# Four places where one stage of a transformer kernel hands over to the next: order of matmuls, norm steps and operand splits changed

## The reference

```
def _layer(x, g_pre, g_post, w_in, ..., w_out, row, col):
    h = _rms_norm(x, g_pre)
    proj = jnp.einsum('bsd,de->bse', h, w_in)
    ...                                        # attention heads o_a, o_b, o_c
    y = jnp.einsum('bse,ed->bsd', jnp.concatenate([o_a, o_b, o_c], axis=-1), w_out)
    return x + _rms_norm(y, g_post)
```

## Time and profile before

| | |
|---|---|
| runs | 2911.41, 2913.14, 2915.44 us; median 2913.14 us |
| profiled execution | 2914.45 us, its span 2912.8 us |
| PE | busy 2877.8 us, 99% of the span |
| PEld / DVE / ACT / POOL | 2472.4 / 2123.5 / 1316.2 / 399.9 us |
| chain that ended last | PE 85%, DVE 5%, DMA 5%, ACT 2% |
| DMA | 620.59 MB, mean 213 GB/s |

### The profile page before, as it was taken

The page is one execution under the profiler, slowest core; times in us unless marked ns, Lnnn a source line. Parts: engine busy times, 40 slices in busy tenths (PEclk is TensorE's granted clock), DMA queues, the critical chain, the costliest instruction groups (busy, mean ns, idle before and its releaser), DMA issues.

```text
span 2912.8 us, 42860 instructions
## 1 busy us (share of the span) xinstructions
PE 2877.8 (99%) x15946; PEld 2472.4 (85%) x15946; DVE 2123.5 (73%) x2854; ACT 1316.2 (45%) x1677; POOL 399.9 (14%) x390
## 2 busy tenths in 40 slices
PE   9999999999999999999999999999999999999998
PEld 7888788888888888988888888888888888887886
DVE  6697776687776857877588787448874488888745
ACT  5443544443543334755355444444444444444433
POOL 1134010133021101020088200000000000000001
PEclk9999999999999999999999999999999999999999
DMA  9867477866568867266455444555445454445543
GB/s 344 306 214 274 177 255 276 303 228 248 194 224 287 302 251 257 80 245 224 168 188 188 187 182 178 189 197 185 179 175 200 187 188 178 174 181 180 193 190 144
DMA packets 100413, 620.59 MB, mean 213 GB/s; under 512 B 11088, under 2 KB 11216, under 8 KB 38096
## 3 DMA queue, kind: packets, MB, share of 16 engines
q1 hardware_dynamic: 71360, 509.88, 47.0%
q0 software_dynamic: 28944, 109.26, 10.6%
HBM read 616.99 MB, written 2.10 MB: 213 GB/s over the span
## 4 chain that ended last, share of the span: by engine, by line
PE 85%; DVE 5%; DMA 5%; ACT 2%; issue 1%; POOL 1%; SPq 0%; POOLq 0%; DVEq 0%; ACTq 0%
PE ps L586 27%; PE ps L1057 17%; PE ps L596 14%; PE ps L540 14%; PE ps L1133 6%; DMA aring<-in_ada 5%; DVE wl L2001 2%; PE ps L1015 1%; DVE aring L2017 1%; ACT BIG L1223 1%; ACT wh L1223 1%; PE ps L778 1%; PE ps L818 0%; PE ps L894 0%; PE ps L698 0%
## 5 line engine op out<-in xcount | busy, mean ns | idle before, releaser
L1223 ACT ACTIVATE wh<-ring 128x2048 fp32r<-128x2048 f32 (+2 forms) x499 | 895.0, 1800 | 1272.7 <-PE ps L596 645.9
L2001 DVE TENSOR_TENSOR wl<-ring,wh 128x2048 fp32r<-128x2048 f32 (+1 forms) x433 | 990.0, 2287 | 482.4 <-ACT stage_h L1223 249.7
L586 PE MATMUL ps<-hhl,wh 128*128 128x512 f32 x3680 | 884.6, 392 | 0.2 <-ACT wh L1223 0.2
L586 PEld LDWEIGHTS ps<-hhl,wh 128*128 128x128 f32 x3680 | 677.1, 189 | 132.5 <-issue 0.9
L596 PEld LDWEIGHTS ps<-hhl,wl 128*128 128x128 f32 x3680 | 471.6, 191 | 19.6 <-DVE wl L2001 1.9
L596 PE MATMUL ps<-hhl,wl 128*128 128x256 f32 x3680 | 477.5, 283 | 0.7 <-DVE wl L2001 0.6
L540 PE MATMUL ps<-wh,hhl 128*128 128x512 f32 (+1 forms) x1728 | 404.1, 386 | 2.5 <-issue 2.3
L540 PEld LDWEIGHTS ps<-wh,hhl 128*128 128x128 f32 x1728 | 319.1, 188 | 65.3 <-issue 3.3
L2017 DVE SCALAR_TENSOR_TENSOR aring<-aring,BIG 128x1024 f32<-128x1024 f32 x192 | 233.9, 1221 | 85.7 <-DMA aring<-in_ada 84.7
L540 PE MATMUL ps<-wl,hhl 128*128 128x512 f32 (+1 forms) x864 | 209.3, 384 | 2.4 <-DVE wl L2001 2.4
L1057 PE MATMUL ps<-wh,stage_h 128*128 128x512 f32 x736 | 196.9, 389 | 0.0
(11 more groups left out here) (327 smaller groups left out, 2585.6 us busy)
## 6 DMA issues: line engine op xcount, KB each, us to landing
ring<-in_stream SPq DMA_DIRECT2D x479, 1024.0 KB, 4.9
aring<-in_ada POOLq DMA_DIRECT2D x192, 512.0 KB, 5.4
X<-in_x SPq DMA_DIRECT2D x4, 512.0 KB, 8.8
BIG<-in_nbr_bias POOLq DMA_DIRECT2D x2, 1024.0 KB, 6.1
BIG<-in_g_post POOLq DMA_DIRECT2D x2, 1024.0 KB, 5.4
out<-X SPq DMA_DIRECT2D x4, 512.0 KB, 2.7
BIG<-in_decays POOLq DMA_DIRECT2D x2, 768.0 KB, 6.0
ring<-in_stream SPq DMA_DIRECT2D x2, 512.0 KB, 6.2
```

What stands on the lines that cost most here:

```text
L586: mm(ps[:, 4 + c, :], wh[:, c % 2, k * P:(k + 1) * P], hhl[:, k, :, :].rearrange("p a b -> p (a b)"), start=(k == 0), stop=False, skip_gro ...
L1223: return nc.scalar.activation(o, i, func, **kw)
L2001: return tt(blocks(wl[:, c % 2, :], cols), blocks(ring[:, c, :], cols), blocks(wh[:, c % 2, :].bitcast(F32), cols), ALU.subtract)
```

## The change

- In the last unit of the output projections of all three seams (2) to (4) the matmuls are ordered by token tile: 8 with wh and 4 with wl for tile 0, then the same for tile 1; a signal `tile_full` after the first 12. ACT and DVE take tile 0 at that signal. At seam (4) such a signal existed after 20 of 24.
- `mean_steps` has two fused steps per tile, one after another, in place of four with pieces of the X update between them; the X update stands behind it. In `prenorm` of seam (3) only block 0 of X is normed first, and PE transposes one quarter, runs nine filler matmuls and the first gate product, and then transposes the second quarter.
- Layer starts: the first 16 wh matmuls run on halves of a quarter (`first_slice`).
- DVE makes the low part of the next group's first weights one step later: after that step's modulation at seams (2) and (3), after the last X update at seam (4). At seam (4) the modulation of step 14 of 16 moves to step 12, so that step 12 has two and the last two steps have none.
- At seam (4) ACT squares X before it makes the second query unit's wh, block 3 of Xn is scaled on POOL in place of ACT, DVE norms block 2 behind the first shift, and `up_pair` begins with 16 matmuls of 256 columns that need hh alone or hl for a quarter.
- Filler matmuls: 8 to 5 at the start, 20 to 15, 32 to 23 (and nine later), 6 to 3.

```diff
-            def rows_slice(g, s, pair, cols, place, first, end):
+            def rows_slice(g, s, pair, cols, place, first, end, by_tile=False, by_pair=False):
...
-                    if n == 16:
+                    if n == (8 if by_tile else 16):
                         split(g, s)
-                    t, kk, j = (n // 8, n // 2 % 4, n % 2) if n < 16 else (n // 4 % 2, n % 4, 2)
+                    if by_tile:
+                        t, kk, j = (n // 12, n % 12 // 2, n % 2) if n % 12 < 8 else (n // 12, n % 12 - 8, 2)
...
+            def first_slice(g, pair, cols, place, l):
+                for half in range(2):
+                    pe.wait_ge(nh_done, l * 8 + half + 1)
...
+                    rows_slice(g, 0, pair, cols, place, 8 * half, 8 * half + 4, by_pair=True)
+                    pe.wait_ge(nl_done, l * 8 + half + 1)
+                    settle()
+                    rows_slice(g, 0, pair, cols, place, 8 * half + 4, 8 * half + 8, by_pair=True)
+                    if half == 0:
+                        transposed(l, 1)
+                rows_slice(g, 0, pair, cols, place, 16, 24).then_inc(unit_done, 1)
...
-                        elif tile is not None and s == R - 1:
-                            rows_slice(g, s, pair, cols, place, 0, 20).then_inc(tile, 1)
-                            rows_slice(g, s, pair, cols, place, 20, 24).then_inc(unit_done, 1)
+                        if tile is not None and s == R - 1:
+                            rows_slice(g, s, pair, cols, place, 0, 12, by_tile=True).then_inc(tile, 1)
+                            rows_slice(g, s, pair, cols, place, 12, 24, by_tile=True).then_inc(unit_done, 1)
...
             transposed(LAYERS, 0, TM2_BANKS, Xn)
-            transposed(LAYERS, 1, TM2_BANKS, Xn)
+            keep_awake(9, 7)
             pe.wait_ge(c2_ready, 16)
             gates(0)
+            transposed(LAYERS, 1, TM2_BANKS, Xn)
...
-            def mean_steps(l):
-                st(tt(part_a, gsum3, yr, ALU.mult))
...
+            def mean_steps():
+                for t in range(T):
+                    st(stt(part_a[:, t:t + 1], gsum3[:, t:t + 1], yr[:, t:t + 1], xsum3[:, t:t + 1], ALU.mult, ALU.add))
                 st.done()
...
+                for t in range(T):
+                    st(stt(xmean[:, t:t + 1], part_a[:, t:t + 1], yr[:, t:t + 1], xmean[:, t:t + 1], ALU.mult, ALU.add))
...
             for j in range(WO_G * R):
-                if j > 1:
+                if 1 < j < WO_G * R - 1:
                     next_low(G_WO2 + j // R, j % R)
                 i, c = j // R, j % R
-                for _ in range(0 if j == WO_G * R - 1 else 2 if j in (2, 3, 6, 7, 10) else 1):
+                for _ in range(0 if j >= WO_G * R - 2 else 2 if j in (2, 3, 6, 7, 10, 12) else 1):
                     modulation(A_WO2 // 2, tiles_taken)
...
                 tt(X[:, t, w], X[:, t, w], Y[:, t, w], ALU.add).then_inc(x_done, 1)
+            next_low(G_WO2 + WO_G - 1, R - 1)
             take_modulation(2)
```

More of the change, by code:

```diff
@@ L640, in _ @@
                 transposed(l, 0)
-                keep_awake(5 if l else 8, 2)
+                keep_awake(5, 2)
                 for i in range(TM_G - 2):
@@ L781, in _ @@
                 for i in range(WO_G):
-                    rows_group(gw + i, l * TM_N + (TM_G + i), i % 2, use=None if i else l, place=PLACE, begun=i == 0)
-                keep_awake(20, 7)
-            keep_awake(12, 7)
+                    rows_group(gw + i, l * TM_N + (TM_G + i), i % 2, use=None if i else l, place=PLACE, begun=i == 0,
+                               tile=tile_full if i == WO_G - 1 else None)
+                keep_awake(15, 7)
+            keep_awake(8, 7)
             def gates(part):
@@ L1169, in up_pair @@
                 pe.wait_ge(hi_done, g * R + 2)
-                for part in range(4):
+                pe.wait_ge(hh_done, use * 4 + 1)
+                settle()
+                for side, operand in ((0, hh), (1, hl)):
+                    if side:
+                        operand_part(use, 0)
+                    for c in range(2):
+                        for k in range(4):
+                            mm(ps[:, 4 + c, side * SEQ:(side + 1) * SEQ], wh[:, c, k * P:(k + 1) * P], operand[:, k, :],
+                               start=(k == 0 and side == 0), stop=False, skip_group_check=True)
+                for part in range(1, 4):
                     operand_part(use, part)
@@ L1586, in _ @@
                   accum_out=ypart[:, t, WO_G - 1:WO_G]).then_inc(sq_done, 1)
+            next_high(G_WQ, 0)
             act.wait_ge(g2_full, 1)
@@ L1950, in prenorm @@
                 if weights is None:
-                    for block in range(3):
+                    for block in range(2):
                         normed(block)
                 else:
-                    for block in range(2):
-                        next_block(LAYERS - 1, block)
+                    next_block(LAYERS - 1, 0)
                 def shifted(part):
@@ L1966, in prenorm @@
                 shifted(0)
[L1967 to L1977, removed]
+                if weights is None:
+                    normed(2)
+                    for part in range(4):
+                        if part < 3:
+                            shifted(part + 1)
+                        low_part(parts[part], use, part)
+                else:
+                    x_block(LAYERS - 1, 1)
+                    next_block(LAYERS - 1, 1)
+                    low_part(parts[0], use, 0)
+                    x_block(LAYERS - 1, 2)
+                    shifted(1)
+                    next_block(LAYERS - 1, 2)
+                    low_part(parts[1], use, 1)
+                    x_block(LAYERS - 1, 3)
+                    next_block(LAYERS - 1, 3)
+                    next_low(weights, 0)
+                    shifted(2)
+                    next_low(weights, 1)
+                    shifted(3)
+                    low_part(parts[2], use, 2)
+                    low_part(parts[3], use, 3)
                 dve.wait_ge(hl_done, use * 4 + 4)
```

87 lines of the change are left out of this document (39 added, 48 removed).

## The result

| | before | changed |
|---|---|---|
| runs, same chip | 2913.16 us (2910.38 to 2917.26, 20 runs) | 2916.97 us (2911.81 to 2926.66, 20 runs) |
| profiled execution, span | 2914.45, 2912.8 us | 2913.11, 2911.4 us |

The ratio is 1.0014, interval [1.0008, 1.0021]: 3.8 us more, inside the 0.2% called no change and inside the range, 2.8 us above the predicted 2914.2. The whole interval lies above 1, so the change is slower, by less than 0.2%. The same kernel run again with the experiments gave 1.0012 [1.0004, 1.0021]. The profiled execution (2913.11 us) happens to be a quick one of the changed kernel, so I read the seams in it and not its total. The second profile, of 2917.09 us, lies at that kernel's median.

What follows compares the result with a forecast made beforehand. PE was taken to set the pace inside stages, and a dependent chain at the seams. Terms -1.85, -1.5, 0 and +4.45 gave +1.1 us on the profiled 2914.45, or 2914.2 us in the runs' terms; range 2909.0 to 2918.0.

Steps and rivals of the forecast that it cites:

- Range: Whole kernel: 2909.0 to 2918.0 us, given 0.83, around a predicted 2914.2; a change under 0.2% counted as none.
- Start: Kernel start: first product 0.8 to 0.95 us earlier, lost again at PE's wait at 39 us; 0, bounds -0.95 and +0.5.
- Seam (2): From one stage's last matmul to the next's first product: earlier square and half-quarter products, -1.85 us, bounds -0.65 and -2.1.
- Seam (3): Stage change up to unit 0: square and shorter mean chain gain, extra transposes cost 0.85; -1.5 us, bounds -0.8 and -2.35.
- the square's 0.65: At seam (3): tile 0's square done while PE computes tile 1, so one square fewer after PE's end; gain 0.65 us.
- Seam (4): Output projection's last unit to next products: late last modulation makes PE stand 4.6 us; with X, norm and clock, +4.45 us.
- the "+1": At seam (4), block 3 of Xn on POOL: costs nothing, or +1 us if POOL is twice as slow.
- The clock: At seam (4): PE's granted clock falls after its stand, costing between 0 and 1.7 us; 0.8 taken.
- Step 12: At seam (4): two modulations in this step, yet the weight split behind them is in time for PE by 0.9 us.
- The early tile: Rival at seam (4): last modulation's tile lands in 3.8 to 4.9 us, PE stands 1.3 to 2.3; 2910.6 us, chance 0.18.
- Slower: Rival at seam (4): last tile takes 8.8 us, PE stands 6.2 us, clock falls throughout; 2916.7 us, chance 0.20.
- little from (2) and (3): Rival: these seams gain only 0.65 and 0.8 us because something else ends last; 2916.1 us, chance 0.10.

Runs made afterwards that it cites:

- f4: Kernel before with the change at the start and at seams (2) and (3) alone, seam (4) as before; ratio 0.9985 against the kernel before.
- e1: Changed kernel with seam (4)'s last modulation put back behind the split of the projection's last unit; ratio 0.9993 against the kernel before.
- e3: Changed kernel with block 3 of Xn scaled on ACT again and not on POOL; ratio 0.9999 against the kernel before.
- e2: Kernel before with one edit alone, step 14's modulation moved to step 12 at seam (4); ratio 1.0010 against the kernel before.
- f3: Changed kernel with last modulation back, block 3 on ACT, and seam (4)'s next-group split at step 15 again; ratio 0.9991 against the kernel before.
- g1: Changed kernel with the second modulation of step 12 at step 9 instead; ratio 0.9999 against the kernel before.

## Why the prediction was right or wrong

- **Range**: right. The time lies inside it, and the change is under the 0.2% of the forecast. It is made of gains at (2) and (3) and a loss at (4), as forecast, but +3.8 and not +1.1. That the sum came so close has luck in it. By the times of f4 the gains are 4.4 us for 3.35 and the loss at (4) is about 8 for 4.45, each with an interval of some us; two errors of opposite sign nearly cancel.
- **Start**, 0: right. It is 0.2 in the first profile, and from 0.3 earlier to 0.7 later in the eleven profiles with the new start. PE's wait at 39 us grew to 0.81 to 2.12, for about 1.4.
- **Seam (2)**, -1.85: right in size and in its parts: -2.1 with the tile at hand, of which 0.74 is gained up to the first transposes (for 0.65) and 1.36 from there to the first product (for 1.2). With a late tile it is -0.9 to -1.8, and of that the prediction had nothing.
- **Seam (3)**, -1.5: mis-sized, -0.4 to -0.6, outside its bounds of -0.8 and -2.35. The term that failed is the square's 0.65: I followed the split to its place behind a modulation and did not ask whether that modulation waits for a tile, which is what I did ask at seam (4). With no tile wait (e1) the seam gave -1.37, and the mean steps started 2.87 after the unit's end for 3.63. The mean chain (1.6 shorter, for 1.75), the gate product 3.4 after the transposes and the extra transposes came as worked out.
- **Seam (4)**, +4.45: +4.4 in the quick profile, +6.4 in the one at the median. The first agreement is chance, since the parts have other sizes. From the last unit's start to X done it is +2.4, not +3.2: the tile took 5.65 us to land (5.6 to 6.7 in four profiles) and not 7.2, and PE stood 3.4 to 3.7, not 4.6. From X to the norm it is +1.15, not +0.7. DVE's list of split and small steps ended 2.8 us after X, as worked out, but it was not the last: POOL's small step beside the moved split (1.32 us for 0.19) came after it, and the norm began 3.3 after X. From the norm on it is +0.8, not -0.25: block 3 on POOL was the "+1" that I had put at nothing, and e3 shows -0.14 without it. I had bounded POOL's own time and not what it does to DVE. The clock cost nothing in one profile and 1.6 in the other, for 0.8.
- **Step 12**: I had its two modulations leave PE's split in time by 0.9. So it was in the changed kernel's two profiles, but in e2 and e3 PE waited 1.22 and 1.10 us in that unit.
- **The early tile** (3.8 to 4.9 us): not seen for the last tile, which took 5.65 us though DVE was idle at its issue (1323.90) until 1324.06 and again from 1327.5 on. The tile before it, issued at 1320.56, was used after a wait at 1324.06, so it landed in 3.5, though DVE worked without a break from before its issue until 1323.17. The two came the other way round from what DVE's idle time alone would give. The rival's place in the sum, a stand of 1.3 to 2.3 us, did not occur.
- **Slower** and **little from (2) and (3)** name the measured time best (2916.7 and 2916.1 for 2916.97). Neither happened as told. Of the first only the clock came, in one of two profiles, with a stand of 3.7 and not 6.2; of the second only the smaller gain at (3). I gave them 0.30 together.
- **The sum of the seams** doesn't give the time of a profile. In the quick profile of the changed kernel the four places add up to +1.7 us and the execution is 1.3 quicker than before's; in the second they add up to +4.9 and it is 2.6 slower. The stretch between (3) and (4) is 4.6 and 2.5 us shorter there than in before's profile, and no run says why.

## What to carry to other kernels

Before moving an instruction ahead of another engine's operand, look at what its own input waits for: an instruction timed by a DMA carries that DMA's spread to all that stands behind it, and here it was harmless only where nobody waited. A finer order of matmuls makes results earlier only if the operands are early too; it also halved the time that hides a late one, from 16 matmuls to eight. And a step given to GpSimd is priced by what VectorE does beside it, on both sides.

## What was not expected of the hardware

- A GpSimd step of 128x2 numbers took 1.32 us (1341.75, ends 1343.07) beside a VectorE split that ended at 1343.02, and 0.19 us without one; when the split moved (f3) the long step moved with it. The Trainium skill (SBUF — State Buffer, "SBUF: two separate sides") says that a VectorE instruction with two SBUF inputs and a GpSimd one that reads SBUF exclude each other for a whole instruction. The end times agree, here and in f3.
- Scaling 128x512 numbers on VectorE took 0.42 us a piece, and 0.72 while GpSimd did the same work (1.76 us a piece). That is slower and not blocked for a whole instruction: a piece that waited for a whole GpSimd one would take over 1.76 us, and the longest took 0.93.
- A stand of 3.4 to 3.7 us was followed by a granted clock below 1.00 in two profiles (0.68 above, 0.58 in e3) and by 1.00 in the third, the changed kernel's first. Behind g1's stand of 2.90 us it was 0.63. So the length of the stand alone did not decide it. e3 and the changed kernel:

```profile
1337.78:1341.20 3.42, 3.42 (x9) 2.75 (x10) 1.27 (x2) 0.91 (x3) 0.58 (x3) 0.58 0.63 216
```

```profile
1335.44:1338.80 3.36, 3.36 (x15) 2.78 (x16) 1.39 (x2) 1.59 (x5) 0.58 (x3) 1.00 0.62 202
```
